# Delta-rule inverse of a mixer stage: five levels on 32-wide diagonal blocks, two levels as off-diagonal blocks

## What is computed

```python
def chunk_gated_delta_rule(q, k, v, g, beta):
    ...
    kb = kc * bc[..., None]
    lower = jnp.where(strict, jnp.einsum("nbhcd,nbhsd->nbhcs", kb, kc) * decay, 0.0)
    rhs = jnp.concatenate([vc * bc[..., None], kb * jnp.exp(gc)[..., None]], axis=-1)
    sol = lax.linalg.triangular_solve(lower, rhs, left_side=True, lower=True, unit_diagonal=True)
    u, w = sol[..., :Dv], sol[..., Dv:]
    def step(S, xs):
        v_new = u_i - jnp.einsum("bhcd,bhdv->bhcv", w_i, S)
        attn = jnp.einsum("bhcd,bhsd->bhcs", q_i, k_i) * d_i
        ...
```

## Time and profile before

| what | value |
|---|---|
| median of 3 runs | 3207.45 us (3206.36 to 3208.13) |
| the profiled execution | 3207.47 us, span 3205.7 us |
| mean granted clock | 0.927 |
| TensorE busy | 2869.8 us, 90% of the span |
| VectorE, ScalarE busy | 1459.7 us (46%), 779.5 us (24%) |
| time of the transfers' packets | 54.3% of 16 engines' span |

### The profile page before, as it was taken

One profiled execution on the slowest core, in us unless ns is written; L12 is line 12 of the kernel. 1 busy time (PEld: TensorE's weight loads), 2 busy tenths in 40 slices (PEclk: granted clock), 3 DMA queues, 4 the chain that ended last, 5 costly groups with the idle time before them and its releaser, 6 DMA issues.

```text
span 3205.7 us, 43344 instructions
## 1 busy us (share of the span) xinstructions
PE 2869.8 (90%) x17606; PEld 2067.1 (64%) x17606; DVE 1459.7 (46%) x3256; ACT 779.5 (24%) x1481; POOL 0.2 (0%) x4
## 2 busy tenths in 40 slices
PE   5999876899899987689999989999999978999998
PEld 4998765799899876679966664333336666333333
DVE  3886445378687443545423332333332532333333
ACT  3331232333333223133223211111101241111010
POOL 0000000000000000000000000000000000000000
PEclk9999787999999977899998878999999988999999
DMA  8776210176577411025421116999995021999997
GB/s 331 280 272 238 79 53 1 53 261 265 193 270 272 174 66 40 1 79 197 179 98 40 53 53 255 427 428 427 427 427 202 31 106 67 384 428 427 427 428 318
DMA packets 71727, 701.80 MB, mean 219 GB/s; under 512 B 8672, under 2 KB 11104, under 8 KB 11232
## 3 DMA queue, kind: packets, MB, share of 16 engines
q1 hardware_dynamic: 71520, 698.91, 54.3%
HBM read 697.84 MB, written 1.05 MB: 218 GB/s over the span
## 4 chain that ended last, share of the span: by engine, by line
PE 49%; DMA 4%; DVE 2%; ACT 2%; issue 1%; DVEq 0%; ACTq 0%; SPq 0%
PE ps L1158 12%; PE ps L761 8%; PE ps L1179 6%; PE ps L1196 4%; DMA ring<-slabs 4%; PE ps L755 3%; PE ps L1374 2%; PE ps L1375 2%; PE ps L1376 2%; PE ps L1128 2%; PE ps L947 1%; DVE x L2649 1%; PE ps L1326 1%; PE ps L915 1%; PE ps L919 1%; PE ps L1167 1%
## 5 line engine op out<-in xcount | busy, mean ns | idle before, releaser
L1374 PE MATMUL ps<-arena_parts 128*128 128x256 f32 x2112 | 604.2, 286 | 24.1 <-DVE arena_parts L2896 24.1
L1375 PE MATMUL ps<-arena_parts 128*128 128x256 f32 x2112 | 600.2, 284 | 0.0
L1376 PE MATMUL ps<-arena_parts,ring_parts 128*128 128x256 f32 x2112 | 599.1, 284 | 0.0
L1158 PE MATMUL ps<-ring,arena 128*64 128x512 f32 x2048 | 472.9, 604 | 4.9 <-ACT arena L1841 4.9
L761 PE MATMUL ps<-h,ring 128*128 128x256 f32 (+1 forms) x1792 | 440.5, 406 | 27.0 <-DVE h L2279 10.0
L1374 PEld LDWEIGHTS ps<-arena_parts 128*128 128x128 f32 x2112 | 404.6, 192 | 25.5 <-issue 25.3
L761 PEld LDWEIGHTS ps<-h,ring 128*128 128x128 f32 x1792 | 357.1, 202 | 93.2 <-issue 11.3
L1376 PEld LDWEIGHTS ps<-arena_parts,ring_parts 128*128 128x128 f32 x2112 | 404.0, 191 | 0.0
L1375 PEld LDWEIGHTS ps<-arena_parts 128*128 128x128 f32 x2112 | 403.1, 191 | 0.3
L2812 DVE TENSOR_TENSOR ring_parts<-ring,arena_parts 128x2048 fp32r<-128x2048 f32 x132 | 299.1, 2289 | 70.0 <-ACT arena_parts L1545 69.9
L1545 ACT CAST arena_parts<-ring 128x2048 fp32r<-128x2048 f32 x132 | 249.1, 1904 | 298.2 <-DMA ring<-slabs 286.2
(11 more groups left out here) (356 smaller groups left out, 2658.0 us busy)
## 6 DMA issues: line engine op xcount, KB each, us to landing
ring<-slabs SPq DMA_DIRECT2D x192, 2048.0 KB, 14.9
ring<-slabs SPq DMA_DIRECT2D x278, 1024.0 KB, 5.3
constants<-const SPq DMA_DIRECT2D x1, 1372.5 KB, 7.3
x<-xT SPq DMA_DIRECT2D x1, 1024.0 KB, 9.7
outT<-x SPq DMA_DIRECT2D x1, 1024.0 KB, 4.7
vectors<-vec SPq DMA_DIRECT2D x1, 747.5 KB, 4.4
ring<-slabs SPq DMA_DIRECT2D x2, 128.0 KB, 3.6
arena<-pos SPq DMA_DIRECT2D x1, 128.0 KB, 7.5
```

Source lines behind the costliest of these rows:

```text
L1158: mm = nc.tensor.matmul(ps[W * hh:W * hh + W, e % 2, :], xe[:, e % 2, 4 * k + c], wt[:, c], start=(k == 0 and c == 0), stop=(k == 1 and c ...
L1374: nc.tensor.matmul(out, w_hi, v_hi, start=start, stop=False, skip_group_check=True)
L1375: nc.tensor.matmul(out, w_hi, v_lo, start=False, stop=False, skip_group_check=True)
L1376: return nc.tensor.matmul(out, w_lo, v_hi, start=False, stop=stop, skip_group_check=True)
```

## The change

The first five levels (sizes 1 to 16) never leave the 32x32 blocks on the diagonal. The new code keeps only these, in compact tiles of 128 x (8 x 32): `ddc` (the diagonal blocks of `dd`), `uc`, `tc`, `pc`. Each product of a level becomes 32 matmuls of 32x32 (8 matrices, 4 blocks), the block c reading and writing partitions 32c to 32c+31, all in one PSUM bank. Level 0 needs no second and third product: with unit blocks they are `p` and its transpose, so `uc = I - p` and `tc = I - low`. Level 5 forms only the two 32x32 off-diagonal blocks of each matrix, level 6 the one 64x64 block, and they are written into zeroed `uu` and `tri`. The masks shrink from 7 x 128 to 5 x 32 columns, `qk` moves ahead of the end of level 5, `turn_outputs` and `take_outputs` from level 2 to 3, `nsa_root` from 1 to 2, `qe` behind level 4. `nsa_square` gains a wait on VectorE's own earlier reduction.

```diff
-                        ("rope", P), ("lev", LEVELS * P), ("near", 6 * 32), ("cneg", 2 * NCMP),
+                        ("rope", P), ("low", 5 * 32), ("near", 6 * 32), ("cneg", 2 * NCMP),
...
+    out["low"] = np.concatenate([near(m) for m in lev[:5]], axis=1)
...
-        UU, PPP, LO = 0, 1024, 2048
+        UU, PC, LOW, DDC, UC, TC = 0, 1024, 1536, 2048, 2304, 2560
+        low_at = lambda lev: view(LOW + 256 * (lev % 2), 8, 32)
+        blocks = [slice(32 * b, 32 * b + 32) for b in range(4)]
...
-                            mm = nc.tensor.matmul(ps[:, t, i * P:(i + 1) * P], lo[:, p], uu[:, p], start=True, stop=True)
...
+                dd, tri, uu = view(LL, 8, P), view(TT, 8, P), view(UU, 8, P)
+                uc, tc, pc = view(UC, 8, 32), view(TC, 8, 32), view(PC, 8, 32)
+                eye = cst("near", 0, 32)
+
+                def small(b, c, p):
+                    return ps[c, b, 32 * p:32 * p + 32]
+
+                for lev in range(5):
+                    await_("dve", q, "lo", lev)
+                    if lev == 0:
+                        await_("dve", q, "kbe", 1)
+                    else:
+                        await_("dve", q, "u", lev - 1)
+                    for p in range(8):
+                        for c in blocks:
+                            mm = nc.tensor.matmul(small(lev % 2, c, p), low_at(lev)[c, p], uc[c, p] if lev else eye[c],
                                                   start=True, stop=True)
-                        mark(mm, q, "up", lev, t)
-                        if lev < LEVELS - 1:
-                            for i in range(GH):
-                                p = GH * t + i
-                                mm = nc.tensor.matmul(ps[:, 4 + t, i * P:(i + 1) * P], pp[:, p], tri[:, p],
-                                                      start=True, stop=True)
-                            mark(mm, q, "tp", lev, t)
-                    if lev == 2:
+                    mark(mm, q, "p", lev)
+                    if lev == 0:
+                        await_("dve", q, "vb", 1)
+                        continue
+                    await_("act", q, "p", lev)
+                    await_("dve", q, "t", lev - 1)
+                    for p in range(8):
+                        for c in blocks:
+                            mm = nc.tensor.matmul(small(2, c, p), tc[c, p], pc[c, p], start=True, stop=True)
+                    mark(mm, q, "up", lev)
+                    for p in range(8):
+                        for c in blocks:
+                            mm = nc.tensor.matmul(small(3, c, p), pc[c, p], tc[c, p], start=True, stop=True)
+                    mark(mm, q, "tp", lev)
+                    if lev == 3:
                         turn_outputs(q, ("mix", l))
...
+                await_("dve", q, "u", 4)
+                for p in range(8):
+                    for c in (0, 64):
+                        mm = nc.tensor.matmul(small(1, slice(c, c + 32), p), dd[c + 32:c + 64, p, c:c + 32],
+                                              uc[c + 32:c + 64, p], start=True, stop=True)
+                mark(mm, q, "p", 5)
+                await_("act", q, "y_att", 1)
                 for t in range(2):
-                    await_("dve", q, "l", t)
                     for i in range(GH):
                         mm = nc.tensor.matmul(ps[:, 6 + t, i * P:(i + 1) * P], qo[:, 4 + i, t * P:(t + 1) * P],
                                               qo[:, i, t * P:(t + 1) * P], start=True, stop=True)
                     mark(mm, q, "qk", t)
+                await_("act", q, "p", 5)
+                await_("dve", q, "t", 4)
+                for p in range(8):
+                    for c in (slice(0, 32), slice(64, 96)):
+                        mm = nc.tensor.matmul(small(2, c, p), tc[c, p], pc[c, p], start=True, stop=True)
+                mark(mm, q, "up", 5)
+                for p in range(8):
+                    mm = nc.tensor.matmul(small(3, slice(32, 64), p), pc[0:32, p], tc[0:32, p], start=True, stop=True)
+                mark(mm, q, "tp", 5)
+                await_("act", q, "wide")
+                for p in range(8):
+                    mm = nc.tensor.matmul(ps[0:64, 0, 64 * p:64 * p + 64], dd[64:128, p, 0:64], uu[64:128, p, 64:128],
+                                          start=True, stop=True)
+                mark(mm, q, "p", 6)
+                await_("act", q, "p", 6)
+                await_("dve", q, "t", 5)
+                for p in range(8):
+                    mm = nc.tensor.matmul(ps[0:64, 1, 64 * p:64 * p + 64], tri[0:64, p, 0:64],
+                                          view(PC, 8, 64)[0:64, p], start=True, stop=True)
+                mark(mm, q, "up", 6)
...
+                uu, uc, pc = view(UU, 8, P), view(UC, 8, 32), view(PC, 8, 32)
+                for lev in range(1, 5):
+                    await_("pe", q, "p", lev)
+                    if lev > 1:
+                        await_("pe", q, "tp", lev - 1)
+                    mark(nc.scalar.copy(pc, ps[:, lev % 2, 0:256].rearrange("p (a n) -> p a n", a=8)), q, "p", lev)
+                    if lev == 2:
                         nsa_root(q)
-                    if lev == 2:
+                    if lev == 3:
                         take_outputs(q, ("mix", l))
+                eight = lambda b, c: ps[c, b, 0:256].rearrange("p (a n) -> p a n", a=8)
+                await_("pe", q, "p", 5)
+                await_("pe", q, "tp", 4)
+                for c in (slice(0, 32), slice(64, 96)):
+                    ins = nc.scalar.copy(pc[c], eight(1, c))
+                mark(ins, q, "p", 5)
+                await_("dve", q, "u", 4)
+                await_("dve", q, "zero")
+                for b, c in enumerate(blocks):
+                    nc.scalar.copy(uu[c, :, c], uc[c])
+                await_("pe", q, "up", 5)
+                for c in (64, 0):
+                    ins = nc.scalar.activation(uu[c:c + 32, :, c + 32:c + 64], eight(2, slice(c, c + 32)), ACT.Copy, scale=-1.0)
+                    if c:
+                        mark(ins, q, "wide")
+                mark(ins, q, "wide0")
+                await_("pe", q, "p", 6)
+                mark(nc.scalar.copy(view(PC, 8, 64)[0:64], ps[0:64, 0, :].rearrange("p (a n) -> p a n", a=8)), q, "p", 6)
...
+                ddc, uc, tc = view(DDC, 8, 32), view(UC, 8, 32), view(TC, 8, 32)
+                near8 = lambda v: v.rearrange("p (a n) -> p a n", a=1).to_broadcast([P, 8, 32])
+                eye = near8(cst("near", 0, 32))
+                eight = lambda b: ps[:, b, 0:256].rearrange("p (a n) -> p a n", a=8)
+                egr = view(QE, 8, P)
+                await_("dve", q, "l", 1)
+                for c in blocks:
+                    ins = nc.vector.tensor_copy(ddc[c], dd[c, :, c])
+                mark(ins, q, "ddc")
+
+                def masked(lev):
+                    if lev >= 2:
+                        await_("pe", q, "p", lev - 2)
+                    mark(nc.vector.tensor_tensor(low_at(lev), ddc, near8(cst("low", 32 * lev, 32)), ALU.mult),
+                         q, "lo", lev)
+
+                await_("dve", q, "ddc")
+                masked(0)
+                await_("dve", q, "lo", 0)
+                mark(nc.vector.tensor_tensor(tc, eye, low_at(0), ALU.subtract), q, "t", 0)
+                masked(1)
+                await_("pe", q, "p", 0)
+                mark(nc.vector.tensor_tensor(uc, eye, eight(0), ALU.subtract), q, "u", 0)
+                for lev in range(1, 5):
+                    if lev < 4:
+                        await_("dve", q, "t", 0)
+                        masked(lev + 1)
+                    if lev < 3:
+                        s4 = slice(4 * lev - 4, 4 * lev)
+                        await_("act", q, "dect", lev - 1)
+                        mark(nc.vector.tensor_tensor(dect[:, s4], dect[:, s4], up4, ALU.mult), q, "dect", lev - 1)
+                        nsa_square(q, lev - 1)
+                    elif lev == 3:
+                        nc.vector.memset(uu, 0.0)
+                        mark(nc.vector.memset(tri[0:64], 0.0), q, "zero")
+                    await_("pe", q, "up", lev)
+                    await_("dve", q, "u", lev - 1)
+                    mark(nc.vector.tensor_tensor(uc, uc, eight(2), ALU.subtract), q, "u", lev)
+                    await_("pe", q, "tp", lev)
+                    await_("dve", q, "t", lev - 1)
+                    mark(nc.vector.tensor_tensor(tc, tc, eight(3), ALU.subtract), q, "t", lev)
+                    if lev == 2:
+                        nsa_scale(q, 0)
+                        nsa_scale(q, 1)
+                for t in range(2):
+                    s4 = slice(4 * t, 4 * t + 4)
+                    await_("act", q, "eg", t)
+                    mark(nc.vector.tensor_tensor(egr[:, s4], egr[:, s4], qo[:, 0:4, t * P:(t + 1) * P], ALU.mult),
+                         q, "qe", t)
+                await_("dve", q, "t", 4)
+                await_("dve", q, "zero")
```

(61 more changed lines are left out.)

32 lines of the change are left out of this document (removed).

## The result

The changed kernel takes **3147.99 us** (median of 4 runs, 3146.75 to 3151.25) where the kernel before takes 3206.9 (4 runs, 3199.96 to 3208.13): ratio 0.9821, 95% interval 0.9809 to 0.9834. That is faster by 59 us, 1.8%, where 68 were forecast (3139, range 3114 to 3165). The profiled execution took 3146.75 us around a span of 3145.0.

A forecast was written before the change was run, and what follows sets the result against it. Bound: a serial chain of stages where TensorE is busy or waited for, including two inverses of 66.9 us. Gain 2 x (66.9 - 29.4 - 4.0) + 0.9 = 67.9 us off 3207.45 gives 3139 us, range 3114 to 3165.

The forecast's parts named there:

- Its own signs: Trace marks of being right: inverse 27 to 32 us, bursts 0.7 to 1.1, levels 3 to 4.2, clock near 0.5, earlier start.
- D: Rival: same mechanism, but 32-partition chains, late VectorE or instruction supply cost 5 to 12 us more per inverse; 3150 to 3165, chance 0.11.
- Total 3.1 + 15.35 + 11.0 = 29.4 us: One new inverse at 1.2 GHz: entry with level 0, levels 1 to 4, then tail, against 66.9 us before.
- Units: Prices of single instructions, such as 64 small records in 1.08 us at clock 0.50 and 0.76 at 1.00.
- B: Rival: diagonal tiles run one after another, 0.028 to 0.056 us a record; mostly 3180 in total, chance 0.12.
- C: Rival: small matmuls not hidden behind their own weight loads, 0.11 us a record, +86 us per inverse; 3312, chance 0.05.
- u is about 1.0 late: Level 3 of the inverse: VectorE's nsa_scale, mask product and two memsets delay u by about 1.0 us; level 4.15 us.
- Level 4, transposes +1.0: Level 4 of the inverse: p(4) stands behind the 8 transposes of turn_outputs, adding 1.0 us; level 4.1 us.
- Tail: End of the inverse, from waiting for tp(4) through level 6: 11.0 us, with p(6) and up(6) 1.9 us each.
- A: Rival: the clock stays at 2.4 GHz through the inverse, which takes 22.9 us; 3119 in total, chance 0.20.
- 4.0 per inverse: Products after each inverse: time given back because they start at the low clock, 4.0 us, bounds 0 and 9.
- Start, 0.9: Kernel start: constants smaller by 377 KB let VectorE begin earlier, gain 0.9 us, bounds 0 and 1.0.

The follow-up runs named there:

- Run 3: Changed kernel with the products of levels 0 to 4 issued one diagonal tile at a time, eight heads in turn; 3186.72 us, one run.
- run 5: Changed kernel with the two memsets of uu and tri moved out of level 3, ahead of the gate sums; 3149.91 us, one run.
- run 4: Changed kernel with t written by a VectorE transpose of u, replacing the tp products and level 0's p product; 3139.64 us, ratio 0.9797 to the kernel before.
- run 6: Changed kernel with twelve unread 512-column products in TensorE's idle time ahead of the levels; 3147.52 us, ratio 0.9817 to the kernel before.
- after: The changed kernel itself, as profiled once the change was made; 3147.99 us, ratio 0.9821 to the kernel before.
- run 9: The kernel of run 4 plus 256 unread matmul records on constants per inverse, behind up in levels 1 to 4; 3149.81 us, one run.
- 10: Changed kernel with 736 columns of zeros put back, so the constants have their old size; 3159.26 us, one run.
- run 11: Changed kernel with VectorE transpose, memsets moved, qk and att earlier, fewer copies before p(6), output transposes later, plus unread filler products; 3129.97 us, ratio 0.9755 to before.

## Why the prediction was right, point by point

- **Mechanism and sign: right.** Less its stops the inverse is 34.51 - 4.95 = 29.6 and 36.32 - 7.08 = 29.2 us against 29.4 forecast. That it fits to 0.2 us is in part luck: in the first inverse, less the stops, the entry took 3.4 (3.1), the levels 16.1 (15.35) and the tail 10.0 (11.0), and the errors cancel.
- **Its own signs were half met.** With its stops the inverse is outside the 27 to 32 us named, levels 2 and 3 take 6.55 and 7.05 us and not 3 to 4.2, and the sign given for D, TensorE idle for "issue", is there. Bursts, clock and start came as named.
- **The step that was mis-sized is "Total 3.1 + 15.35 + 11.0 = 29.4 us": it has instruction supply at zero.** Rival D named it, with the 472 matmuls, but only as a price of 5 to 12 us with a chance of 0.11. Measured 5.0 and 7.1 us; its two other parts cost nothing that shows. The sum with what was measured: 2 x (66.94 - 35.42 - 2.82) + 0.8 = 58.2 (means of both stages). The whole is inside the forecast's 3128 to 3150, short of D's 3150, only because other things gave back part of it: the inverses cost 12.0 us more than forecast, the recurrences 2.4 less, and 2.5 went in code that the change doesn't touch. The last is luck.
- **Units: right.** Bursts 1.08 us (1.08), 0.75 at full clock (0.76). The four copies 1.18 (0.99).
- **Do diagonal tiles overlap: yes**, so B and C fall. Run 3 prices the serial case at 0.046 us a record, within B's bounds (0.028 to 0.056) though under the 0.056 that B has for this clock. The Trainium skill, "TensorEngine Tiling (Array Packing)", Restrictions and Gotchas, has row tiles excluded from one bank at a time; this form, tiles that differ in row and column at once, ran in one bank at 0.015 us a record.
- **Level 3, "u is about 1.0 late": counted though hidden.** The memsets do hold VectorE until 527.76, but p(4) stands behind the transposes until 530.39, so this 1.0 and the 1.0 of the transposes run side by side and may not be added (rows of run 5, and run 4, which has no stop).
- **Level 4, transposes +1.0:** they take 1.97 us at the low clock, 1.0 more. The two errors cancel.
- **Tail:** p(6) and up(6) 1.14 and 1.19 us, not 1.9, since the clock was at 1.00 there for a moment, behind qk; in the second inverse 1.14 and 1.97.
- **Clock: right in the main.** 0.50 in the levels but for the end of the second inverse's (A fails; in run 6 the clock falls even when the levels are entered at 1.00). "4.0 per inverse": 3.9 and 1.7, so the second is 2.3 us too high.
- **Start, 0.9:** 0.8 us.

## What to carry to other kernels

When wide products are cut into many small ones, count instructions beside columns. Here a need of 384 TensorE instructions in 3.3 us, level after level, ended in stops "for issue" in the middle of bursts; 256 in 3.27 us for four levels did not. Where a stretch stops like this, a saving elsewhere in it can be swallowed. Take instructions out (a transpose on an idle VectorE for a product, here 28.9 instead of 34.5 us) before shaving waits. Keep neighbours in the instruction order on different tiles: 1.08 us for 64 records in turn, 3.05 us tile by tile.

## What the runs showed of the hardware that was not expected

- Instructions of TensorE come in blocks of 256, one in 3.3 to 4.1 us as the stops of after and of runs 6, 9 and 10 are spaced. In the first inverse of after 602 were issued from its start before a stop, 256 more with a pause of 3.4 us; in its second inverse 436 (218 matmul records) and in run 9 348 (174), so the lead is not a fixed number. What sets the pace is open. The Trainium skill, "Runtime: NRT & Kernel Launch", Instruction fetch mechanics, gives the same block of 256 instructions, and calls the cost of crossing one "mostly hidden"; here it is 5 to 7 us of a 35 us stretch, so the measurement decides.
- 64 records of 32x32 on four diagonal tiles of one bank take 1.08 us in turn and 3.05 us tile by tile, at a granted clock of 0.50.
- A stop of 1.2 to 1.9 us was followed by a fall of the granted clock from 1.00 to 0.50 in both inverses of run 6 and the first of run 11; in the second of run 11 no stop was longer than 0.81 us and it fell too. The fillers in the waits behind the products didn't bring it back: in the first inverse of run 11 it was 0.50 from 524 to 536 with TensorE busy for 11.8 of 12.0 us. What brings it down isn't separated.
